# Opening stage of a transformer layer: value weights loaded by rows in eight chunks, first token tile in halves, products chunk by chunk

## The chip, the cores and the metric

One core of a Trainium2 chip runs one layer of a streaming-encoder trunk (1024 tokens, width 1024). The metric is the device time of one execution in microseconds (us), lower is better. Engines are named as in the profile: PE is TensorE (PEld its weight loads), DVE VectorE, ACT ScalarE, POOL GpSimd, SP SyncE, which issues all the DMA transfers here.

## What the kernel must compute

Only the start of the layer matters here: the normalised tokens `xn`, and the two value projections `va` and `vb` out of one combined input projection. The rest of the layer (attention, output projection, convolutional feed-forward, gate) follows unchanged.

```
def rms_norm(x, g):
    xf = x.astype(jnp.float32)
    y = xf * lax.rsqrt(jnp.mean(xf * xf, axis=-1, keepdims=True) + EPS)
    return (y * g.astype(jnp.float32)).astype(x.dtype)
...
        xn = rms_norm(h, norm_mix[i])
        proj = xn @ w_in[i]
        qa, ka, va, qb, kb, vb = jnp.split(proj, SPLITS, axis=-1)
...
        h = h + jnp.concatenate([oa, ob], axis=-1) @ w_out[i]
        h = h + gated_conv_ffn(rms_norm(h, norm_ffn[i]), w_ffn_in[i], conv_w[i], conv_b[i], w_ffn_out[i])
        gate = jax.nn.sigmoid(rms_norm(h, norm_ple[i]) @ w_ple_gate[i])
        h = h + gate * (p[i] @ w_ple[i])
    return rms_norm(h, norm_final)
```

The value columns are 512 of `vb` (from column 1792) and 128 of `va` (from column 640): 640 columns by 1024 rows of `w_in`, 2.5 MB.

## The kernel before

Every engine has its own program, written out by hand, and semaphores order them. Nothing is scheduled by a planner: the order on an engine is the order of the code in its block.

To keep float32 accuracy, every operand of a matrix product is split in two, `hi` (a rounded copy that ACT makes) and `lo` (the rest, which DVE makes by subtraction, L1185, after ACT's copy L793), and every product is made of three (`SPLIT3`: hi·hi, hi·lo, lo·hi).

The opening works on eight token tiles of 128 tokens, t = 0 to 7. For each, SP loads `x_in`; ACT squares it with a running sum (`square`, L796); DVE makes mean plus epsilon (L1194); POOL takes the power -0.5 (`power`, L687); DVE scales by that and by the gain `g_mix` into `xs0` (L1220); PE transposes `xs0` into PSUM in eight 128x128 pieces (`x_turn0`, L1729); ACT and DVE split the transposed tile into `act_t` (`x_hi0`, `x_lo0`); then PE makes the value products of the tile, 48 matmuls (`v_proj`, L1723: eight blocks k of 128 rows, times three, times two column pieces of 384 and 256). I call the tiles tile 0, tile 1 and so on, and "the products of tile u" is `v_proj(u)`.

The value weights come in five column pieces of 128 columns and all 1024 rows (`load_v`, five DMAs of 512 KB, in pieces of 512 bytes), into buffers that are not yet in use (`raws`). ACT and DVE split each (`split_v`) into `wv`. Since a piece of columns holds all rows, the products of tile 0 can begin on the first three column pieces (`v_proj(0, (0,))` waits for `wv_lo` 3) and go on with the other two (`v_proj(0, (1,))` waits for `wv_lo` 5). Before that PE runs transposes of the identity whose result nobody reads, 28 ahead of the transposes of tile 0 and 36 behind them.

SP's queue holds, in this order: `x_in` of tile 0, `g_mix`, the five weight loads, `x_in` of tile 1, the small tables (`prow` with the convolution's columns, `oneh` and `relb` for the bias table), six small constants, `x_in` of tile 2, the first query/key weight tile (`load_w(0)`, into `w_raw`, which is also the buffer of weight piece 2 and so waits for its split), and the other tiles. The small tables are turned by PE after tile 1's transposes (`cols_t`, `brow_t`) and copied by ACT after tile 0's value copies.

ACT's and DVE's loops run over t and hold at each t: the square (or scaling) of tile t, then, for t of 2 and more, the split of tile t - 1, then the value results of tile t - 2. At t = 0 they also hold the five weight splits and tile 0's split. ACT's square of tile 1 waits for `wv_lo` 4, because its junk output lies where weight piece 3 was landed.

Of the kernel before, what the change touches and what calls it, by code (L numbers as in the profile page):

```python
# [16 lines left out]
ALU = mybir.AluOpType  # L17
# [46 lines left out]
def build(nc, x, p, w_in, w_out, sinks, lambda_q, lambda_k, subln_gain, rel_bias, norm_mix, norm_ffn,  # L64
# [7 lines left out]
    def sb(stack, name, shape, dt=F32):  # L72
        return stack.enter_context(nc.sbuf_tensor(name, shape, dt))
# [3 lines left out]
    def sem(name):  # L77
# [20 lines left out]
    by_type = ExitStack()  # L98
    k_f = sb(by_type, "k_f", [P, 2, SEQ])
    by_type.close()  # L100
# [9 lines left out]
    g_mix = sb(early, "g_mix", [P, D])  # L110
    wv_raw = sb(early, "wv_raw", [P, 2, KD, P])
    prow = sb(early, "prow", [P, P])
# [19 lines left out]
    V_CUT = 3 * P  # L132
    raws = [wv_raw[:, 0], wv_raw[:, 1], w_raw[:, :, :],
            xs0[:, 1, :].rearrange("p (k n) -> p k n", k=KD), k_f[:, 0, :].rearrange("p (k n) -> p k n", k=KD)]
    q_a = wq[:, 4 * D:12 * D].rearrange("p (s l c u q) -> p s l c u q", s=2, l=2, c=NCH, u=2)
# [52 lines left out]
    def blk_there(eng, q, n):  # L188

        eng.wait_ge(wv_loaded[q], (16 if q < 5 else 0) + 16 * n)  # L190

# [212 lines left out]
    def _(sp):  # L404
        sp.dma_start(x_in[:, 0, :], x[0:P, :]).then_inc(x_loaded[0], 16)
        sp.dma_start(g_mix[:, :], row(norm_mix, D)).then_inc(S.gain_in, 16)

        def load_v(r):
            c = VB0 + P * r if r < 4 else VA0
            sp.dma_start(raws[r], w_in_v[:, :, c:c + P]).then_inc(wv_loaded[r], 16)  # L410

        load_v(0)
        load_v(1)
        load_v(2)
        load_v(3)
        load_v(4)
        sp.dma_start(x_in[:, 1, :], x[P:2 * P, :]).then_inc(x_loaded[1], 16)
# [10 lines left out]
        def load_w(j):  # L428
            if j == 0:
                sp.wait_ge(S.wv_lo, 3)  # L430
            else:
                sp.wait_ge(S.w_lo, j)
            at = 0
            for c, n in tiles[j]:
                sp.dma_start(w_raw[:, :, at:at + n], w_in_v[:, :, c:c + n]).then_inc(S.w_loaded, 16)
                at += n

        for t in range(2, NT):
            sp.wait_ge(S.xs0_ready, t - 1)
            sp.dma_start(x_in[:, t % 2, :], x[t * P:(t + 1) * P, :]).then_inc(x_loaded[t % 2], 16)  # L440
            if t == 2:
                load_w(0)

# [4 lines left out]
        load_w(2)  # L448
        sp.wait_ge(S.xs0_ready, NT)
        sp.wait_ge(S.tr0, NT)  # L450
        sp.wait_ge(S.wv_lo, 5)
        sp.wait_ge(S.consts_ready, 1)
# [338 lines left out]
    def _(act):  # L791
# [18 lines left out]
        def x_hi0(t):  # L810
            act.wait_ge(S.tr0, t + 1)
            b = 2 * (t % 2)
            copy(act_t[:, 0, :, t * P:(t + 1) * P], ps[:, b:b + 2, :].rearrange("p b (k n) -> p (b k) n", k=4), S.xhi0)

        for t in range(NT + 2):
            if t < NT:
                act.wait_ge(x_loaded[t % 2], 16 * (t // 2 + 1))
                if t == 1:
                    act.wait_ge(S.wv_lo, 4)
                if t >= 2:  # L820
                    act.wait_ge(S.tr0, t - 1)
# [17 lines left out]
            if t == 2:  # L839
                act.wait_ge(S.cols_t, 1)  # L840
                copy(cols[:, :], ps[:, 7, 0:4 * NF], S.act_self)
                act.wait_ge(S.brow_t, 1)
                copy(brow[:, :], ps[0:AH + BH, 5, 0:NREL], S.brow_ready)

# [330 lines left out]
    def _(dve):  # L1175
# [19 lines left out]

        def split_v(r):
            dve.wait_ge(S.wv_hi, r + 1)
            dst = wv[:, :, :, P * r:P * r + P]
            low(dst[:, 1], raws[r], dst[:, 0], S.wv_lo)

# [4 lines left out]
        def x_lo0(t):  # L1205
            dve.wait_ge(S.xhi0, t + 1)
            b = 2 * (t % 2)
            sl = slice(t * P, (t + 1) * P)
            low(act_t[:, 1, :, sl], ps[:, b:b + 2, :].rearrange("p b (k n) -> p (b k) n", k=4),
                act_t[:, 0, :, sl], S.xlo0)  # L1210

        for t in range(NT + 2):
            if t < NT:
                dve.wait_ge(S.sq0, t + 1)
                mean_eps(stat[:, 56 + t % 2:57 + t % 2], stat[:, t:t + 1], D, S.ms0)
            if t == 0:
                dve.wait_ge(S.gain_in, 16)
            if t < NT:
                dve.wait_ge(S.pow0, t + 1)
                nc.vector.scalar_tensor_tensor(out=xs0[:, t % 2, :], in0=x_in[:, t % 2, :],  # L1220
                                               scalar=stat[:, 8 + t:9 + t], in1=g_mix[:, :],
                                               op0=ALU.mult, op1=ALU.mult).then_inc(S.xs0_ready, 1)
            if t == 0:
                split_v(0)
                x_lo0(0)
                for r in range(1, 5):
                    split_v(r)
            if t == 5:
                split_w(0)
            if 2 <= t <= NT:  # L1230
# [490 lines left out]
    def _(pe):  # L1721
# [486 lines left out]
```

## Time and profile before

| | |
|---|---|
| runs of the kernel before | 1227.92, 1230.97, 1232.18 us; median 1230.97 |
| profiled execution, first to last instruction (span) | 1229.7 us, the one time that the profiled execution has |
| PE busy | 1197.1 us, 97% of the span |
| DVE, ACT, POOL busy | 867.3, 517.8, 250.2 us |
| mean granted TensorE clock | 0.992 of full speed |

The span runs from the first to the last instruction of one profiled execution; the runs are timed on the device without the profiler's records. The busy share is an average over the whole layer; what the opening costs is read from a timeline of its own. "PEclk" in the profile is the share of full speed that TensorE's clock was granted: 1.00 is 2.4 GHz, 0.50 is 1.2 GHz. Instruction times in the timeline are those of a group of like instructions that follow one another: its start, its length, and in brackets how long the engine had been idle and what ended that.

### The profile page before, as it was taken

Reading aid. Unit: us, or ns where it says so; the run is one execution under the profiler, and the core shown is the slowest. Engines: PE = TensorE matmul, PEld = TensorE weight load, DVE = VectorE, ACT = ScalarE, POOL = GpSimd, SP = SyncE. Lnnn points to the kernel's source line nnn. Section 1 sums busy time; section 2 is a strip of 40 time slices with the busy share of each in tenths; the row PEclk is TensorE's granted clock in tenths of the full one; section 3 lists DMA queues with packets and bytes.
Section 4 is the critical chain, followed back from the end, with each engine's and each line's share of the span. In section 5 each row is a group of like instructions: output and inputs, shape, how many; then the busy total and the mean of one; then the engine's idle time right before and its main releaser. Section 6 shows DMA issues by size and latency. Waiting matters only on the chain.

```text
span 1229.7 us, 17128 instructions
## 1 busy us (share of the span) xinstructions
PE 1197.1 (97%) x6167; PEld 1001.8 (81%) x6167; DVE 867.3 (71%) x1514; ACT 517.8 (42%) x1045; POOL 250.2 (20%) x291
## 2 busy tenths in 40 slices
PE   8999999999888999999999999999999999999997
PEld 7998887788676888888888888888888888888886
DVE  5433786877886577877787777877777999964443
ACT  4312665565655224433343343343344444733321
POOL 0000000344455122232332323323210000000000
PEclk9999999999899999999999999999999999999999
DMA  7464233111831512242322333233499533620101
GB/s 217 89 90 91 50 89 76 42 40 69 222 139 42 164 52 81 82 128 94 121 87 89 125 103 112 95 94 112 146 345 312 172 95 103 225 75 26 43 35 51
DMA packets 127916, 136.08 MB, mean 111 GB/s; under 512 B 15714, under 2 KB 93274, under 8 KB 127770
## 3 DMA queue, kind: packets, MB, share of 16 engines
q1 hardware_dynamic: 127834, 135.00, 36.1%
q8 instruction: 49, 0.80, 0.3%
q14 instruction: 33, 0.27, 0.1%
HBM read 96.77 MB, written 37.22 MB: 109 GB/s over the span
## 4 chain that ended last, share of the span: by engine, by line
PE 61%; issue 4%; DVE 2%; POOL 1%; ACT 1%; POOLq 0%; DVEq 0%; ACTq 0%
PE ps L1723 60%; PE ps L1729 1%; DVE xs L1474 1%; DVE h L1469 0%; DVE conv L1410 0%; POOL stat L687 0%; ACT xs L796 0%; DVE act_t L1185 0%; POOL stat L706 0%; POOL bias_a L712 0%; POOL more_f L714 0%; PE ps L2118 0%; ACT wbuf L793 0%; POOL o_t L709 0%; DVE h L1688 0%
## 5 line engine op out<-in xcount | busy, mean ns | idle before, releaser
L1723 PE MATMUL ps<-act_t,wbuf 128*128 128x512 f32 x1200 | 280.1, 389 | 0.5 <-DVE a_buf L1499 0.5
L1723 PEld LDWEIGHTS ps<-act_t,wbuf 128*128 128x128 f32 x1200 | 225.2, 188 | 47.5 <-DVE a_buf L1499 0.8
L1723 PE MATMUL ps<-wbuf 128*128 128x512 f32 x912 | 214.8, 390 | 0.0
L1723 PEld LDWEIGHTS ps<-wbuf 128*128 128x128 f32 x912 | 170.6, 188 | 35.1
L1723 PE MATMUL ps<-act_t,wq 128*128 128x512 f32 x624 | 152.2, 396 | 3.6 <-DVE wq L1187 3.0
L1723 PEld LDWEIGHTS ps<-act_t,wq 128*128 128x128 f32 x624 | 114.3, 188 | 30.8 <-issue 7.5
L687 POOL TENSOR_TENSOR stat<-stat 128x1 f32<-128x1 f32 x32 | 17.6, 549 | 420.9 <-DVE stat L1194 420.9
L793 ACT ACTIVATE wbuf<-raw 128x512 fp32r<-128x512 f32 (+1 forms) x107 | 69.0, 646 | 73.9 <-PE ps L1723 63.8
L1723 PE MATMUL ps<-hx,wbuf 128*128 128x512 f32 x408 | 95.7, 389 | 0.0
L1185 DVE TENSOR_TENSOR wbuf<-raw,wbuf 128x512 fp32r<-128x512 f32 (+1 forms) x107 | 87.4, 818 | 11.5 <-ACT wbuf L793 11.2
L1723 PEld LDWEIGHTS ps<-hx,wbuf 128*128 128x128 f32 x408 | 76.5, 188 | 15.9
L875 ACT ACTIVATE e_t<-ps,small 128x128 f32<-128x128 f32 (+7 forms) x64 | 47.3, 740 | 63.4 <-DVE small L1314 62.3
L793 ACT ACTIVATE wbuf<-xs 128x512 fp32r<-128x512 f32 x66 | 39.8, 624 | 71.9 <-DVE xs L1410 54.2
L1723 PE MATMUL ps<-wbuf,act_t 128*128 128x512 f32 x288 | 69.6, 395 | 0.0
L1723 PEld LDWEIGHTS ps<-wbuf,act_t 128*128 128x128 f32 x288 | 52.9, 188 | 10.5
L1723 PE MATMUL ps<-wq,act_t 128*128 128x384 f32 (+1 forms) x384 | 59.5, 315 | 1.5 <-DVE wq L1185 1.5
L1723 PEld LDWEIGHTS ps<-wq,act_t 128*128 128x128 f32 x384 | 57.9, 193 | 2.0 <-issue 1.7
L1723 PE MATMUL ps<-act_t,more 128*128 128x512 f32 x240 | 56.8, 389 | 0.0
L714 POOL TENSOR_TENSOR wbuf_f<-wbuf_f 128x512 f32<-128x512 f32 x33 | 52.2, 1581 | 18.6 <-DVE wbuf_f L1553 15.6
L1185 DVE TENSOR_TENSOR a_t<-ps,a_t 128x512 fp32r<-128x512 f32 (+4 forms) x64 | 44.6, 715 | 15.4 <-ACT a_t L793 15.3
L1723 PEld LDWEIGHTS ps<-act_t,more 128*128 128x128 f32 x240 | 45.0, 188 | 9.4
L1185 DVE TENSOR_TENSOR wbuf<-xs,wbuf 128x512 fp32r<-128x512 f32 x66 | 50.3, 762 | 0.5
(208 smaller groups left out, 1962.8 us busy)
## 6 DMA issues: line engine op xcount, KB each, us to landing
u_ops<-wbuf_f SPq DMA_DIRECT2D x77, 256.0 KB, 2.2
raw<-u_ops SPq DMA_DIRECT2D x77, 256.0 KB, 2.7
raw<-in_w_ffn_in SPq DMA_DIRECT2D x33, 512.0 KB, 3.8
g_ffn<-in_w_ffn_in SPq DMA_DIRECT2D x11, 512.0 KB, 3.9
act_f<-in_w_ffn_out SPq DMA_DIRECT2D x21, 256.0 KB, 4.3
w_raw<-in_w_in SPq DMA_DIRECT2D x10, 512.0 KB, 4.4
wbuf_f<-in_w_ffn_out SPq DMA_DIRECT2D x18, 256.0 KB, 5.9
x_in<-in_x SPq DMA_DIRECT2D x8, 512.0 KB, 3.8
```

The lines of the kernel that those rows point to most:

```text
L687: nc.gpsimd.tensor_tensor(dst, src, stat[:, 63:64], ALU.pow).then_inc(done, 1)
L714: nc.gpsimd.tensor_tensor(dst, a, b, ALU.subtract).then_inc(done, 1)
L793: nc.scalar.activation(dst, src, ACT.Copy, scale=scale).then_inc(done, 1)
L875: nc.scalar.activation(e_t[:, pr, m, 0:w], psf[:, at:at + w], ACT.Exp, scale=-1.0, bias=small[:, o + 2 + m:o + 3 + m], accum_out=small[:, ...
L1185: ins = nc.vector.tensor_tensor(dst, src, hi.bitcast(F32), ALU.subtract)
L1474: nc.vector.scalar_tensor_tensor(out=xs[:, i % 2, :], in0=h[:, t, :], scalar=stat[:, 8 + i:9 + i], in1=g_ffn[:, :], op0=ALU.mult, op1=ALU. ...
L1723: return nc.tensor.matmul(dst, lhs, rhs, start=start, stop=stop)
L1729: ins = nc.tensor.transpose(psf[:, bank * HALF + k * P:bank * HALF + (k + 1) * P], src[:, k * P:(k + 1) * P], ident[:, :])
```

## The change

The value weights are loaded by rows: eight chunks of 128 rows, each chunk in two DMAs (512 columns of `vb`, 256 KB, and 128 columns of `va`, 64 KB), into eight buffers of 640 columns (`v_raws`). The small tables move ahead of the weights in SP's queue, `x_in` of tile 1 stands between the second and the third chunk, and `x_in` of tile 2 stands right behind the last chunk, ahead of the six constants. `load_w(0)` no longer waits, since `w_raw` is no longer used for value weights.

ACT and DVE split chunk by chunk (640 columns instead of 1024, eight times instead of five). Tile 0 is scaled, transposed and split in two halves (`first_hi`, `first_lo`). Chunks 0 to 2 are split at t = 0 and chunks 3 to 7 at t = 1, behind tile 1's scaling; tile 1's split stands between those of chunks 5 and 6. The copies of the small tables move from t = 2 to t = 0 on ACT.

On PE 24 transposes of the identity stay and the 36 go; the small tables are turned before tile 0; the products of tile 0 run block by block, each waiting for its chunk, and tile 1's transposes stand ahead of block 6.

```diff
-    raws = [wv_raw[:, 0], wv_raw[:, 1], w_raw[:, :, :],
-            xs0[:, 1, :].rearrange("p (k n) -> p k n", k=KD), k_f[:, 0, :].rearrange("p (k n) -> p k n", k=KD)]
+    v_half = v_f[:, NT * 2 * P:2 * NT * 2 * P]
+    v_raws = [wv_raw[:, 0], wv_raw[:, 1]] + [x[:, NV * i:NV * (i + 1)] for x in (v_half, k_f) for i in range(3)]
...
-        def load_v(r):
-            c = VB0 + P * r if r < 4 else VA0
-            sp.dma_start(raws[r], w_in_v[:, :, c:c + P]).then_inc(wv_loaded[r], 16)
...
+        def load_v(k):
+            sp.dma_start(v_raws[k][:, 0:4 * P], w_in[k * P:(k + 1) * P, VB0:VB0 + 4 * P]).then_inc(wv_loaded[k], 16)
+            sp.dma_start(v_raws[k][:, 4 * P:NV], w_in[k * P:(k + 1) * P, VA0:VA0 + P]).then_inc(wv_loaded[k], 16)
...
+        load_v(0)
+        load_v(1)
+        load_x(1)
+        for k in range(2, KD):
+            load_v(k)
+        sp.wait_ge(S.xs0_ready, 2)
+        load_x(2)
...
             if t == 0:
                 split_v(0)
-                x_hi0(0)
-                for r in range(1, 5):
-                    split_v(r)
+                first_hi(0)
+                first_hi(1)
+                split_v(1)
+                act.wait_ge(S.cols_t, 1)
+                copy(cols[:, :], ps[:, 7, 0:4 * NF], S.act_self)
+                act.wait_ge(S.brow_t, 1)
+                copy(brow[:, :], ps[0:AH + BH, 5, 0:NREL], S.brow_ready)
+                split_v(2)
+            if t == 1:
+                split_v(3)
+                split_v(4)
+                split_v(5)
+                x_hi0(1)
+                split_v(6)
+                split_v(7)
...
-        def v_proj(u, cuts):
+        def v_proj(u):
+            cuts = (0, 1)
             for k in range(KD):
+                if u == 0:
+                    if k == 6:
+                        x_turn0(1)
+                    pe.wait_ge(S.wv_lo, k + 1)
+                    if k == 0:
+                        pe.wait_ge(S.xlo0, 1)
+                    if k == 4:
+                        pe.wait_ge(S.xlo0, 2)
...
-        for _ in range(28):
+        for _ in range(24):
             nc.tensor.transpose(ps[:, 7, 0:P], ident[:, :], ident[:, :])
-        x_turn0(0)
-        for _ in range(36):
-            nc.tensor.transpose(ps[:, 7, 0:P], ident[:, :], ident[:, :])
-        pe.wait_ge(S.xlo0, 1)
-        pe.wait_ge(S.wv_lo, 3)
-        v_proj(0, (0,))
-        pe.wait_ge(S.wv_lo, 5)
-        v_proj(0, (1,))
-        x_turn0(1)
         pe.wait_ge(S.cols_in, 32)
...
+        for half in range(2):
+            pe.wait_ge(S.xs0_ready, half + 1)
+            for k in range(4 * half, 4 * half + 4):
+                ins = nc.tensor.transpose(psf[:, k * P:(k + 1) * P], xs0[:, 0, k * P:(k + 1) * P], ident[:, :])
+            ins.then_inc(S.tr0, 1)
+        v_proj(0)
```

DVE's order changes as ACT's does. These are DVE's instructions in the kernel before, from the first mean (`TENSOR_SCALAR stat`) to the split of tile 1; `xs` is the scaled tile `xs0`, the rows that write `wq` are the weight splits (named by the buffer that they read), and those that write `act_t` the token splits.

```order
L1194 TENSOR_SCALAR stat<-stat 128x1 [waits sq0]
L1220 SCALAR_TENSOR_TENSOR xs<-x_in,stat,g_mix 128x1024 [waits pow0,gain_in]
L1185 TENSOR_TENSOR wq<-wv_raw,wq 128x8x128 [waits wv_hi]
L1185 TENSOR_TENSOR act_t<-ps,act_t 128x8x128 [waits xhi0]
L1185 TENSOR_TENSOR wq<-wv_raw,wq 128x8x128 [waits wv_hi]
L1185 TENSOR_TENSOR wq<-w_raw,wq 128x8x128 [waits wv_hi]
L1185 TENSOR_TENSOR wq<-xs,wq 128x8x128 [waits wv_hi]
L1185 TENSOR_TENSOR wq<-k_f,wq 128x8x128 [waits wv_hi]
L1194 TENSOR_SCALAR stat<-stat 128x1 [waits sq0]
L1220 SCALAR_TENSOR_TENSOR xs<-x_in,stat,g_mix 128x1024 [waits pow0]
```

And these are DVE's in the changed kernel, from the third weight split to the scaling of tile 2.

```order
L1199 TENSOR_TENSOR wq<-v_f,wq 128x640 [waits wv_hi]
L1208 TENSOR_SCALAR stat<-stat 128x1 [waits sq0]
L1244 SCALAR_TENSOR_TENSOR xs<-x_in,stat,g_mix 128x1024 [waits pow0]
L1199 TENSOR_TENSOR wq<-v_f,wq 128x640 [waits wv_hi] x2
L1199 TENSOR_TENSOR wq<-k_f,wq 128x640 [waits wv_hi]
L1199 TENSOR_TENSOR act_t<-ps,act_t 128x8x128 [waits xhi0]
L1199 TENSOR_TENSOR wq<-k_f,wq 128x640 [waits wv_hi] x2
L1208 TENSOR_SCALAR stat<-stat 128x1 [waits sq0]
L1244 SCALAR_TENSOR_TENSOR xs<-x_in,stat,g_mix 128x1024 [waits pow0]
```

Before, all weight splits stood ahead of tile 1's mean; now tile 1's mean and scaling stand in their middle, and tile 1's split (the row that writes `act_t`) stands between chunks 5 and 6, ahead of tile 2's scaling instead of behind it. On PE the kernel before had this order at the start (`ident` alone is the transposes that nobody reads; `prow` and `oneh,relb` are the small tables).

```order
L1753 MATMUL ps<-ident 128x128 x28
L1729 MATMUL ps<-ident,xs 128x128 x8
L1756 MATMUL ps<-ident 128x128 x36
L1723 MATMUL ps<-wq,act_t 128x384 x24
L1723 MATMUL ps<-wq,act_t 128x256 x24
L1729 MATMUL ps<-ident,xs 128x128 x8
L1764 MATMUL ps<-ident,prow 128x88
L1723 MATMUL ps<-oneh,relb 12x384
```

The changed kernel has this one; it stops at the first of tile 0's matmuls.

```order
L1794 MATMUL ps<-ident 128x128 x24
L1796 MATMUL ps<-ident,prow 128x88
L1755 MATMUL ps<-oneh,relb 12x384
L1802 MATMUL ps<-ident,xs 128x128 x8
L1755 MATMUL ps<-wq,act_t 128x384
```

The small tables stand ahead of tile 0 now, the 36 transposes are gone, and tile 1's transposes (not in these rows) stand behind 36 of tile 0's 48 matmuls.

## Rows read from the trace of the kernel before

**Rows 1.** The page's first part: span, and PE's busy time.

```profile
span 1229.7 us, 17128 instructions
...
PE 1197.1 (97%) x6167; PEld 1001.8 (81%) x6167; DVE 867.3 (71%) x1514; ACT 517.8 (42%) x1045; POOL 250.2 (20%) x291
```

**Rows 2.** Timeline of PE, 0 to 52 us.

```profile
1.54 5.31 PE L1753 MATMUL ps<-ident 128*128 128x128 f32 x28 [1.54 <-POOL ident L682]
...
14.40 7.30 PE L1723 MATMUL ps<-wq,act_t 128*128 128x384 f32 x48 [1.46 <-DVE wq L1185]
...
25.23 1.09 PE L1729 MATMUL ps<-ident,xs 128*128 128x128 f32 x8 [1.84 <-DVE xs L1220]
26.36 8.78 PE L1723 MATMUL ps<-wq,act_t 128*128 128x384 f32 x48
...
35.77 7.29 PE L1723 MATMUL ps<-wq,act_t 128*128 128x384 f32 x48
...
43.69 7.29 PE L1723 MATMUL ps<-wq,act_t 128*128 128x384 f32 x48
```

**Rows 3.** Timeline of ACT, DVE and POOL, 0 to 27 us.

```profile
4.49 1.06 ACT L796 ACTIVATE xs<-x_in 128x1024 f32<-128x1024 f32 x1 [2.49 <-DMA x_in<-in_x]
...
5.91 0.55 POOL L687 TENSOR_TENSOR stat<-stat 128x1 f32<-128x1 f32 x1 [4.42 <-DVE stat L1194]
...
6.57 1.28 DVE L1220 SCALAR_TENSOR_TENSOR xs<-x_in,stat,g_mix 128x1024 f32<-128x1024 f32 x1 [0.75 <-POOL stat L687]
...
8.31 1.06 ACT L793 ACTIVATE wq<-wv_raw 128x1024 fp32r<-128x1024 f32 x1 [2.68 <-DMA wv_raw<-in_w_in]
...
21.89 1.06 ACT L796 ACTIVATE xs<-x_in 128x1024 f32<-128x1024 f32 x1 [3.76 <-DMA x_in<-in_x]
...
22.95 1.00 ACT L793 ACTIVATE act_t<-ps 128x1024 fp32r<-128x1024 f32 x1
...
23.89 1.28 DVE L1220 SCALAR_TENSOR_TENSOR xs<-x_in,stat,g_mix 128x1024 f32<-128x1024 f32 x1 [0.66 <-POOL stat L687]
...
25.09 1.22 DVE L1185 TENSOR_TENSOR act_t<-ps,act_t 128x1024 fp32r<-128x1024 f32 x1
```

**Rows 4.** Timeline, 87 to 89 us: ACT's copy and DVE's split of 512 columns.

```profile
87.23 0.60 ACT L793 ACTIVATE k_a<-ps 128x512 fp32r<-128x512 f32 x1 [2.27 <-PE ps L1723]
87.86 0.69 DVE L1185 TENSOR_TENSOR k_a<-ps,k_a 128x512 fp32r<-128x512 f32 x1 [2.01 <-ACT k_a L793]
```

**Rows 5.** Transfers from 0 to 100 us: KB each, median us from issue to landing.

```profile
x_in<-in_x SPq DMA_DIRECT2D x8, 512.0 KB, 3.8
...
g_mix<-in_norm_mix SPq DMA_DIRECT2D x1, 512.0 KB, 5.3
...
lqk<-in_lambda_q SPq DMA_DIRECT2D x2, 32.0 KB, 4.0
```

**Rows 6.** SP's queue, 0 to 17 us: start and length of issues.

```profile
1.19 0.41 SPq L406 DMA_DIRECT2D g_mix<-in_norm_mix  x1
...
13.40 0.42 SPq L423 DMA_DIRECT2D lqk<-in_lambda_q  x1
...
16.23 0.43 SPq L440 DMA_DIRECT2D x_in<-in_x  x1
```

**Rows 7.** Stretches: length, busy us (x instructions) by engine, granted clock, DMA share, GB/s.

```profile
10.00:12.00 2.00, 2.00 (x20) 2.00 (x19) 2.00 (x3) 1.29 (x3) 0.00 (x0) 1.00 1.20 291
14.00:16.00 2.00, 1.60 (x9) 1.63 (x10) 1.43 (x2) 1.28 (x2) 0.00 (x0) 1.00 1.10 356
...
24.00:26.00 2.00, 0.77 (x7) 0.78 (x8) 2.00 (x2) 2.00 (x7) 0.00 (x0) 1.00 0.01 2
26.00:28.00 2.00, 1.96 (x9) 1.72 (x8) 1.34 (x6) 1.18 (x3) 0.55 (x1) 0.56 0.76 240
28.00:30.00 2.00, 2.00 (x11) 2.00 (x10) 2.00 (x2) 0.00 (x0) 0.00 (x0) 0.59 0.06 23
...
22.20:23.00 0.80, 0.80 (x7) 0.34 (x5) 0.00 (x0) 0.80 (x3) 0.00 (x0) 1.00 1.04 419
```

More of the change, by code:

```diff
@@ L39 @@
 QB0, KB0, VB0 = 768, 1280, 1792
+NV = 640
 HALF = 512
@@ L98, in build @@
     by_type = ExitStack()
-    k_f = sb(by_type, "k_f", [P, 2, SEQ])
+    k_f = sb(by_type, "k_f", [P, 2 * SEQ])
+    v_f = sb(by_type, "v_f", [P, 2 * NT * 2 * P])
     by_type.close()
@@ L110, in build @@
     g_mix = sb(early, "g_mix", [P, D])
-    wv_raw = sb(early, "wv_raw", [P, 2, KD, P])
+    wv_raw = sb(early, "wv_raw", [P, 2, NV])
     prow = sb(early, "prow", [P, P])
@@ L188, in blk_there @@
     def blk_there(eng, q, n):
-        eng.wait_ge(wv_loaded[q], (16 if q < 5 else 0) + 16 * n)
+        eng.wait_ge(wv_loaded[q], (32 if q < KD else 0) + 16 * n)
     def s_tmp(n, f):
@@ L406, in _ @@
         sp.dma_start(g_mix[:, :], row(norm_mix, D)).then_inc(S.gain_in, 16)
-        def load_v(r):
-            c = VB0 + P * r if r < 4 else VA0
-            sp.dma_start(raws[r], w_in_v[:, :, c:c + P]).then_inc(wv_loaded[r], 16)
[L412 to L417, printed above, removed]
         sp.dma_start(prow[0:3 * NF, :], conv_w.rearrange("c (f p) -> (c f) p", p=P)).then_inc(S.cols_in, 16)
@@ L421, in _, with load_x @@
         sp.dma_start(relb[:, :], rel_bias).then_inc(S.onehot_in, 16)
+        def load_v(k):
+            sp.dma_start(v_raws[k][:, 0:4 * P], w_in[k * P:(k + 1) * P, VB0:VB0 + 4 * P]).then_inc(wv_loaded[k], 16)
+            sp.dma_start(v_raws[k][:, 4 * P:NV], w_in[k * P:(k + 1) * P, VA0:VA0 + P]).then_inc(wv_loaded[k], 16)
+        def load_x(t):
+            sp.dma_start(x_in[:, t % 2, :], x[t * P:(t + 1) * P, :]).then_inc(x_loaded[t % 2], 16)
+        load_v(0)
[5 more added lines that the diff above has]
+        load_x(2)
         for j in range(2):
@@ L428, in load_w @@
         def load_w(j):
-            if j == 0:
-                sp.wait_ge(S.wv_lo, 3)
-            else:
+            if j >= 1:
                 sp.wait_ge(S.w_lo, j)
@@ L436, in load_w @@
                 at += n
[L438 to L442, printed above, removed]
+        load_w(0)
+        for t in range(3, NT):
+            sp.wait_ge(S.xs0_ready, t)
+            load_x(t)
         load_w(1)
@@ L448, in _ @@
         load_w(2)
-        sp.wait_ge(S.xs0_ready, NT)
-        sp.wait_ge(S.tr0, NT)
-        sp.wait_ge(S.wv_lo, 5)
+        sp.wait_ge(S.xs0_ready, NT + 1)
+        sp.wait_ge(S.tr0, NT + 1)
+        sp.wait_ge(S.wv_lo, KD)
         sp.wait_ge(S.consts_ready, 1)
@@ L796, in square, with split_v, first_hi @@
             nc.scalar.activation(junk, src, ACT.Square, accum_out=acc).then_inc(done, 1)
-        def split_v(r):
-            act.wait_ge(wv_loaded[r], 16)
-            copy(wv[:, 0, :, P * r:P * r + P], raws[r], S.wv_hi)
+        def split_v(k):
+            act.wait_ge(wv_loaded[k], 32)
+            copy(wv[:, 0, k, :], v_raws[k], S.wv_hi)
+        def first_hi(half):
+            act.wait_ge(S.tr0, half + 1)
+            copy(act_t[:, 0, 4 * half:4 * half + 4, 0:P], ps[:, half, :].rearrange("p (k n) -> p k n", k=4),
+                 S.xhi0)
         def split_w(j):
@@ L810, in x_hi0 @@
         def x_hi0(t):
-            act.wait_ge(S.tr0, t + 1)
+            act.wait_ge(S.tr0, t + 2)
             b = 2 * (t % 2)
@@ L817, in _ @@
                 act.wait_ge(x_loaded[t % 2], 16 * (t // 2 + 1))
-                if t == 1:
-                    act.wait_ge(S.wv_lo, 4)
                 if t >= 2:
-                    act.wait_ge(S.tr0, t - 1)
+                    act.wait_ge(S.tr0, t)
                 square(x_in[:, t % 2, :], xs0[:, t % 2, :], stat[:, 56 + t % 2:57 + t % 2], S.sq0)
@@ L824, in _ @@
                 split_v(0)
-                x_hi0(0)
-                for r in range(1, 5):
-                    split_v(r)
+                first_hi(0)
[13 more added lines that the diff above has]
+                split_v(7)
             if t == 5:
                 split_w(0)
-            if 2 <= t <= NT:
+            if 3 <= t <= NT:
                 x_hi0(t - 1)
@@ L838, in _ @@
                 copy(v_a[:, u, 0, :], ps[:, 6 + u % 2, P:2 * P], S.vhi)
[L839 to L843, printed above, removed]
         def unit_hi(u):
@@ L1194, in mean_eps, with split_v, first_lo @@
             nc.vector.tensor_scalar(dst, src, 1.0 / width, EPS, ALU.mult, ALU.add).then_inc(done, 1)
[L1196 to L1199, printed above, removed]
+        def split_v(k):
+            dve.wait_ge(S.wv_hi, k + 1)
+            low(wv[:, 1, k, :], v_raws[k], wv[:, 0, k, :], S.wv_lo)
+        def first_lo(half):
+            dve.wait_ge(S.xhi0, half + 1)
+            ks = slice(4 * half, 4 * half + 4)
+            low(act_t[:, 1, ks, 0:P], ps[:, half, :].rearrange("p (k n) -> p k n", k=4), act_t[:, 0, ks, 0:P],
+                S.xlo0)
         def split_w(j):
@@ L1205, in x_lo0 @@
         def x_lo0(t):
-            dve.wait_ge(S.xhi0, t + 1)
+            dve.wait_ge(S.xhi0, t + 2)
             b = 2 * (t % 2)
@@ L1217, in _ @@
                 dve.wait_ge(S.gain_in, 16)
-            if t < NT:
+                dve.wait_ge(S.pow0, 1)
+                for half in range(2):
+                    nc.vector.scalar_tensor_tensor(out=xs0[:, 0, HALF_X[half]], in0=x_in[:, 0, HALF_X[half]],
+                                                   scalar=stat[:, 8:9], in1=g_mix[:, HALF_X[half]], op0=ALU.mult,
+                                                   op1=ALU.mult).then_inc(S.xs0_ready, 1)
+            if 1 <= t < NT:
                 dve.wait_ge(S.pow0, t + 1)
@@ L1224, in _ @@
                 split_v(0)
-                x_lo0(0)
-                for r in range(1, 5):
-                    split_v(r)
+                first_lo(0)
+                first_lo(1)
+                split_v(1)
+                split_v(2)
+            if t == 1:
+                split_v(3)
+                split_v(4)
+                split_v(5)
+                x_lo0(1)
+                split_v(6)
+                split_v(7)
             if t == 5:
                 split_w(0)
-            if 2 <= t <= NT:
+            if 3 <= t <= NT:
                 x_lo0(t - 1)
@@ L1733, in x_turn0 @@
         def x_turn0(t):
-            pe.wait_ge(S.xs0_ready, t + 1)
+            pe.wait_ge(S.xs0_ready, t + 2)
             if t >= 2:
-                pe.wait_ge(S.xlo0, t - 1)
+                pe.wait_ge(S.xlo0, t)
             turn8(xs0[:, t % 2, :], 2 * (t % 2), S.tr0)
-        def v_proj(u, cuts):
+        def v_proj(u):
+            cuts = (0, 1)
             for k in range(KD):
+                if u == 0:
[6 more added lines that the diff above has]
+                        pe.wait_ge(S.xlo0, 2)
                 for n, (a, b) in enumerate(SPLIT3):
@@ L1766, in _ @@
         mm(ps[0:AH + BH, 5, 0:NREL], relb[:, :], oneh[:, :], True, True).then_inc(S.brow_t, 1)
+        for half in range(2):
+            pe.wait_ge(S.xs0_ready, half + 1)
[3 more added lines that the diff above has]
+        v_proj(0)
         for t in range(2, NT + 1):
@@ L1770, in _ @@
             u = t - 1
-            pe.wait_ge(S.xlo0, u + 1)
+            pe.wait_ge(S.xlo0, u + 2)
             if u == 1:
@@ L1776, in _ @@
                 pe.wait_ge(S.vlo, u - 1)
-            v_proj(u, (0, 1))
+            v_proj(u)
         def unit(u, part=None):
@@ L1783, in unit @@
                 if u == 0:
-                    pe.wait_ge(S.xlo0, NT)
+                    pe.wait_ge(S.xlo0, NT + 1)
                 if u < FIRST_UNITS:
```

## The prediction

> **What bounds the kernel now.** I read the page first: PE is busy for 1197.1 of 1229.7 us [rows 1], so nearly everything waits for PE, and time can be won only where PE is not at work or works slowly. PE's timeline of the opening came next [rows 2]. PE makes transposes that nobody reads until the weights are there, starts the products of tile 0 at 14.40 and those of tile 1 at 26.36, after an idle stretch of 1.84 us behind DVE. From tile 2 on it is in step: tile 2 starts at 35.77 and tile 3 at 43.69, 7.92 us apart, and ACT and DVE are idle for most of it. So all that the opening can win or lose is how much earlier or later **the products of tile 2 start than 35.77 us**. What follows is PE's own work and shifts as a whole.
>
> The clock is the third thing to see. Tile 1's products took 8.78 us, tile 2's 7.29 [rows 2]; the stretches show why: granted 1.00 at 24 to 26 us while PE idled, 0.56 and 0.59 in the next two [rows 7]. From 26.36 to 35.77 is 9.41 us instead of 7.92: this fall cost 1.5 us. The earlier gap, 1.46 us ahead of 14.40, was followed by a granted 1.00.
>
> Last, ACT's and DVE's timeline of the same place [rows 3] tells what PE waited for: `x_in` of tile 2, issued at 16.23 [rows 6], let its square start only at 21.89, 5.7 us later where the median of such loads is 3.8 [rows 5]; scaling followed at 23.89, PE's transposes at 25.23. Tile 1's split on DVE (25.09 to 26.31) ended just before tile 1's products.
>
> **The change, part by part.**
>
> *Transfers.* The bytes are the same, in larger pieces for four fifths of them. `g_mix` has landed by 1.19 + 5.3 = 6.5 us as before [rows 5, 6]. The small tables are 92 KB, 0.2 to 0.3 us at the rates below, so 6.8. Pieces of 512 bytes came at 291 GB/s (10 to 12 us), pieces of 4 KB at 419 (22.2 to 23.0) [rows 7]; the trace has no piece of 2 KB from HBM alone. A chunk of 328 KB is thus 0.78 to 1.13 us; I take 0.9, since a fifth of it is in the small pieces and the rest between. Chunk 0 is there at 7.7, chunk 1 at 8.6, tile 1 (512 KB, 1.25) at 9.9, chunks 2 to 7 at 10.8, 11.7, 12.6, 13.5, 14.4, 15.3, tile 2 at 16.6: 5 us sooner than it was. Issuing does not hold this up: 0.43 for each [rows 6], some 0.9 a chunk, and the first chunk's are out near 4 us.
>
> *Splits.* 1024 columns cost ACT 1.06 and DVE 1.22 [rows 3], 512 cost 0.60 and 0.69 [rows 4], so 640 cost about 0.71 and 0.82. Back to back each engine gives back about 0.1 of that (ACT's square at 21.89 of 1.06 and its accumulator's read are followed by the next copy at 22.95). Eight chunks are 8 x 0.72 = 5.8 us on DVE against 5 x 1.13 = 5.7: the work stays, its order changes.
>
> *The chain, step by step* (estimates from those rows; PE's part at full clock, 7.12 us between 35.77 and the next transposes, or 0.89 a block of six matmuls). Scaling of tile 0 begins at 6.57 as now, in halves of about 0.7, so it ends at 8.0. PE has the small tables turned by about 7.8, and tile 0's halves at 8.4 and 8.8. ACT: chunk 0 7.8 to 8.5, halves to 9.5, chunk 1 to 10.1, the two table copies to 10.6, chunk 2 10.9 to 11.6, square of tile 1 11.5 to 12.65, chunks 3, 4, 5 to 14.5. DVE: chunk 0 to 9.4, halves to 10.6, chunk 1 to 11.3, chunk 2 11.65 to 12.5; then tile 1's mean waits for the square (12.7), POOL's power takes it to 13.55 (0.66 from its start to the scaling [rows 3]), scaling to 14.8, chunks 3, 4, 5 to 15.6, 16.3, 17.05. PE: blocks 0, 1, 2 at 10.0, 11.35, 12.5; block 3 at 15.6, then 4 and 5 without a gap to 18.3.
>
> Here stands the new wait. Tile 1's transposes come behind block 5, and tile 1's split stands ahead of chunks 6 and 7 on ACT and DVE. Queued behind it are those two splits, and behind them tile 2's square, mean and scaling; PE waits for all of these in turn. From the end of block 5: transposes 1.05, ACT's copy 1.0 [rows 3], DVE's subtraction 1.22, two chunks 1.5, mean and power 0.8, scaling 1.3, transposes until the first product 0.9: 7.8 us, plus about 0.1 for handing over. In that time PE has two blocks and two sets of transposes to do, 3.9 us. So tile 1's products start at 18.3 + 7.9 = 26.2 and tile 2's at 34.1, **if the clock holds**. Against 35.77 that is 1.65 us won.
>
> *The clock.* It won't hold, I think. Blocks 0 to 2 come with gaps, and from 13.4 to 15.6 PE is idle for 2.2 us: longer than the 1.84 that was followed by the fall, while 1.46 was not. The 36 transposes that kept PE at work are gone. If the fall comes near 16 us and ends with block 4, blocks 3 to 5 end at 19.85 instead of 18.3 (half speed, as in 26 to 30 us [rows 7]: block 4 costs 1.6 to 1.8 instead of 0.89), and all behind them moves by 1.55: tile 1 at 27.75, tile 2 at 35.7. Against 35.77 that is nothing. What the change wins, the 1.5 us of slow clock in tile 1 and the late `x_in` of tile 2, it gives back in the chain that PE now waits for and in a slow clock one tile sooner.
>
> *The rest.* `load_w(0)` without its wait, `cols` and `brow` sooner: all were ready long before their users, so nothing. The small constants come later by the one load of tile 2 and are read only after tile 7's values. Blocks of tile 0 in another order of the same 48 matmuls: nothing.
>
> **The sum.** -1.65 + 1.55 = -0.1 us at tile 2. The profiled span of 1229.7 becomes 1229.6; the runs' median is 1230.97, so 1.3 us more than that profile, which I keep: **1230.9 us**, no change. The three runs shown lie 4.3 us apart, and about 0.3% (3.7 us) is what a measurement can tell from none.
>
> **The rivals.**
>
> *The clock holds* (or falls where no product stands): tile 2 at 34.1, 1229.3 us; still within 0.3%. For it speaks that PE was granted 1.00 after a gap of 1.46 and that blocks 0 to 2 are some work; against it the 2.2 us. A floor beneath it: DVE's work from 6.57 on with no wait but the chain above, 1.35 + 0.75 + 1.25 + 1.45 (tile 0, three chunks) + 0.85 + 1.2 (tile 1's scaling) + 2.2 (three chunks) + 3.0 (block 5, transposes, copy) + 1.15 + 1.5 + 0.85 + 1.2 + 0.9, ends at 24.2, so tile 2 at 32.1 at best: 3.7 us won, 1227.3 us. Only this floor would count as faster, and it needs early chunks, tile 1's square ahead of chunk 2, and a full clock at once.
>
> *The clock falls twice or stays low* (the other side: slower). PE is idle again between tile 1's transposes and block 6, 3 us (20.9 to 24.0), and half idle until tile 1. A second fall that reaches tile 1's transposes costs about what it cost before, 1.4 us: 1232.4. If the clock is low throughout from 16.0 until tile 1 has begun: blocks 3 to 5 end at 20.6, both sets of transposes cost 2 us instead of 1, and tile 1 starts at 30.5 with 1.5 us of slow products, so tile 2 at 39.9: 4.1 us lost, 1235.1. It decides at block 5: if that and tile 1's transposes still run at the low clock, slower it is. The Trainium skill's page "TensorE: Matmul & The Clock Gate", section "HAM oscillation — how this bites in real kernels", says that bursts of matmuls with waits for data between them fall back to half clock burst after burst. By that rule this is the likely case; the trace agrees with one fall after a wait, and shows no series of them here.
>
> *Chunks later.* At 1.13 us a chunk, chunk 2 comes at 11.4 and chunk 5 at 14.8; the square of tile 1 and all behind it move by 0.6, the rest is hidden behind DVE: 1231.5. Were transfers served one at a time, each for the 3.7 to 4.0 us of small ones, sixteen of them would put chunk 5 past 45 us and the kernel past 1255. Against it: the 32 KB loads are issued 0.5 apart and land within 4.0 [rows 5, 6]. The skill's "DMA: Bandwidth & Descriptors", section "Rules for kernel authors", asks for 1 MiB a transfer and calls those under 64 KB mostly overhead; by it 64 KB and 256 KB instead of 512 KB speak against this change. The trace shows overhead that overlaps.
>
> **How the numbers follow.** One fall, nothing won: 0.4. Clock holds, or nearly: 0.25. A second fall, or later chunks (1231.5 to 1232.4): 0.2. Low throughout (1235): 0.07. The floor (1227.3): 0.07. Transfers in series: 0.01. Together faster by over 0.3% 0.09, slower 0.11, the rest between, with the runs' own spread of some 2 us either way on top. The range of 8 in 10 takes the floor and the low clock nearly in: 1227.5 to 1234.5.
>
> **What would show it.** In the changed kernel's trace: chunk splits on ACT at 7.8 and then never late for data after chunk 2; DVE idle about 3 us between chunk 5 and tile 1's split; PE idle before block 3 and between tile 1's transposes and block 6; granted clock 0.5 near 16 to 19 us; tile 2's products at 34 to 37 us. Wrong it would be if tile 2 starts before 32.5 (a chain shorter than I worked out), after 39 (clock or transfers), or if the time moves elsewhere: the clock's other falls in the middle of the kernel may shift with it, which I put at nothing.

## The result, and the profile after

| | before | after |
|---|---|---|
| median of 9 runs each, us | 1229.29 (1227.69 to 1232.18) | 1232.88 (1229.94 to 1235.13) |
| ratio, 95% interval | | 1.0024 [1.0012, 1.0035] |
| span of the profiled execution, us | 1229.7 | 1230.0 |
| products of tile 2 start (profiled execution), us | 35.77 | 37.49 |

The change costs 0.24%, some 3 us. I had forecast no change. The page's first part has the same shape as before [rows 1]:

```profile
span 1230.0 us, 17068 instructions
...
PE 1192.8 (97%) x6127; PEld 996.9 (81%) x6127; DVE 868.8 (71%) x1519; ACT 517.8 (42%) x1049; POOL 249.6 (20%) x291
```

PE's timeline of the opening, which answers to [rows 2] (start, length, group, idle time before it):

```profile
10.41 3.49 PE L1755 MATMUL ps<-wq,act_t 128*128 128x384 f32 x18 [1.07 <-DVE act_t L1199]
15.81 4.45 PE L1755 MATMUL ps<-wq,act_t 128*128 128x384 f32 x18 [1.91 <-DVE wq L1199]
20.10 1.03 PE L1761 MATMUL ps<-ident,xs 128*128 128x128 f32 x8
24.23 3.57 PE L1755 MATMUL ps<-wq,act_t 128*128 128x384 f32 x12 [3.10 <-DVE wq L1199]
27.60 1.91 PE L1761 MATMUL ps<-ident,xs 128*128 128x128 f32 x8
29.16 7.70 PE L1755 MATMUL ps<-wq,act_t 128*128 128x384 f32 x48
...
37.49 7.29 PE L1755 MATMUL ps<-wq,act_t 128*128 128x384 f32 x48
...
45.41 7.29 PE L1755 MATMUL ps<-wq,act_t 128*128 128x384 f32 x48
```

The first row is blocks 0 to 2 of tile 0 (18 of 48 matmuls), the second blocks 3 to 5, the third tile 1's transposes, the fourth blocks 6 and 7. Two things are to be seen: PE is idle for 3.10 us ahead of block 6, waiting for DVE; and the twelve matmuls behind it, which take 2.03 us in a kernel further down, took 3.57. The stretches say why (columns as in [rows 7]; the clock is the third number from the right):

```profile
10.00:12.00 2.00, 1.47 (x8) 1.24 (x9) 1.72 (x4) 2.00 (x6) 0.00 (x0) 1.00 1.07 382
...
14.00:16.00 2.00, 0.19 (x1) 0.19 (x2) 2.00 (x3) 0.77 (x2) 0.00 (x0) 1.00 1.07 372
16.00:18.00 2.00, 2.00 (x10) 2.00 (x10) 1.23 (x2) 0.00 (x0) 0.00 (x0) 0.60 1.04 242
18.00:20.00 2.00, 2.00 (x10) 2.00 (x9) 0.00 (x0) 0.00 (x0) 0.00 (x0) 0.54 0.93 320
20.00:22.00 2.00, 1.13 (x10) 0.89 (x8) 0.00 (x0) 0.83 (x1) 0.00 (x0) 1.00 0.04 16
22.00:24.00 2.00, 0.00 (x0) 0.00 (x0) 1.77 (x2) 2.00 (x4) 0.00 (x0) 0.81 0.00 0
24.00:26.00 2.00, 1.76 (x6) 1.77 (x7) 1.34 (x4) 0.48 (x2) 0.55 (x1) 0.50 0.00 0
26.00:28.00 2.00, 2.00 (x9) 2.00 (x9) 0.93 (x1) 0.16 (x1) 0.00 (x0) 0.50 0.11 16
28.00:30.00 2.00, 2.00 (x11) 2.00 (x10) 1.11 (x4) 2.00 (x6) 0.04 (x1) 0.50 0.71 254
```

Each of PE's two idle stretches (before block 3, before block 6) brings a fall of the clock: to 0.60 and 0.54 in the first case, to 0.50 in the second. The second sets in while PE is still idle (0.81 at 22 to 24 us) and lasts into tile 1's products. DVE's timeline shows what PE waited for:

```profile
16.41 0.82 DVE L1199 TENSOR_TENSOR wq<-k_f,wq 128x640 fp32r<-128x640 f32 x1
22.23 1.23 DVE L1199 TENSOR_TENSOR act_t<-ps,act_t 128x1024 fp32r<-128x1024 f32 x1 [5.00 <-ACT act_t L797]
23.37 1.55 DVE L1199 TENSOR_TENSOR wq<-k_f,wq 128x640 fp32r<-128x640 f32 x2
```

Chunk 5's split ends at 17.2; then DVE stands still for 5.00 us, since the next in its order is tile 1's split, which needs ACT's copy, which needs PE's transposes, which stand behind block 5. Chunks 6 and 7 (the last row), long landed, wait behind it.

### The profile page after: what moved, and what is told of

Same layout as the page of the kernel before. It is cut to its first block, busy times and chain, and to the rows that moved or that the text cites. A ratio compares the mean times of both kernels' runs of the same rounds, so it can differ in the third digit from the quotient of the medians.

```text
span 1230.0 us, 17068 instructions
## 1 busy us (share of the span) xinstructions
PE 1192.8 (97%) x6127; PEld 996.9 (81%) x6127; DVE 868.8 (71%) x1519; ACT 517.8 (42%) x1049; POOL 249.6 (20%) x291
## 4 chain that ended last, share of the span: by engine, by line
PE 61%; issue 4%; DVE 2%; POOL 1%; ACT 1%; POOLq 0%; DVEq 0%; ACTq 0%
PE ps L1755 60%; PE ps L1761 1%; DVE xs L1506 1%; DVE h L1501 0%; DVE conv L1442 0%; POOL stat L691 0%; ACT xs L800 0%; DVE act_t L1199 0%; POOL stat L710 0%; POOL bias_a L716 0%; POOL more_f L718 0%; PE ps L2156 0%; ACT wbuf L797 0%; POOL o_t L713 0%; DVE conv L1717 0%
## 5 line engine op out<-in xcount | busy, mean ns | idle before, releaser
L797 ACT ACTIVATE wbuf<-xs 128x512 fp32r<-128x512 f32 x66 | 39.9, 624 | 71.6 <-DVE xs L1442 54.2
L1755 PE MATMUL ps<-wq,act_t 128*128 128x384 f32 (+1 forms) x384 | 62.6, 323 | 6.2 <-DVE wq L1199 5.0
```

Of the source, the lines that this page charges most:

```text
L797: nc.scalar.activation(dst, src, ACT.Copy, scale=scale).then_inc(done, 1)
L1755: return nc.tensor.matmul(dst, lhs, rhs, start=start, stop=stop)
```

## The experiments

Each kernel was timed in rounds against the kernel before on the same chip. "Tile 2" below is where the products of tile 2 start in that kernel's own profiled execution.

**before_again: the kernel before, again** (no edit).

> The kernel before, unchanged, so that its executions are seen more than once. Theory 1 (the profiled execution of before was a late one): here the products of tile 2 start at 32.5 to 34.5 us instead of 35.77, with no fall of the clock at 26 us, and the ratio is 1.000. Theory 2 (that profile was typical, and the changed kernel loses by its own later start alone): tile 2 starts at 35.5 to 36.0 again.

Ratio 0.9997 [0.9986, 1.0009], profiled span 1227.3. PE's timeline:

```profile
14.44 7.27 PE L1723 MATMUL ps<-wq,act_t 128*128 128x384 f32 x48 [1.51 <-DVE wq L1185]
...
24.14 1.09 PE L1729 MATMUL ps<-ident,xs 128*128 128x128 f32 x8 [0.74 <-DVE xs L1220]
25.28 7.31 PE L1723 MATMUL ps<-wq,act_t 128*128 128x384 f32 x48
...
33.22 7.29 PE L1723 MATMUL ps<-wq,act_t 128*128 128x384 f32 x48
```

And ACT's square of tile 2:

```profile
20.80 1.06 ACT L796 ACTIVATE xs<-x_in 128x1024 f32<-128x1024 f32 x1 [2.45 <-DMA x_in<-in_x]
```

Theory 1 holds. Tile 1's products took 7.31 us, not 8.78, and tile 2 starts at 33.22, 2.55 us sooner than in [rows 2]. The load of tile 2 let its square start at 20.80 instead of 21.89 [rows 3], PE's idle gap was 0.74 instead of 1.84, and no fall followed. The spans of all executions say which of the two profiles is the typical one: over the 67 later executions of the kernel before, the median is 1227.3 us, this profile's own, and only 7 reach the 1229.7 of the first.

**before_x2_sooner: the kernel before with tile 2's load ahead of the small constants.**

```diff
+        sp.wait_ge(S.xs0_ready, 1)
+        sp.dma_start(x_in[:, 0, :], x[2 * P:3 * P, :]).then_inc(x_loaded[0], 16)
         for j in range(2):
             sp.dma_start(lqk[:, j], row(lambda_q[j], HD)).then_inc(S.consts_in, 16)
```

(Further down, the loop that issued it before leaves it out.)

> The kernel before with one edit: tile 2's load stands ahead of the six small constants, as in the changed kernel. Theory 1 (the late landing at 21.9 us and the fall of the clock behind it were a chance of that one execution): ratio 0.999 to 1.001. Theory 2 (the late landing is there in most executions): tile 1's products start at 24.5 to 25.2 without a fall of the clock, tile 2's near 33, ratio 0.997 to 0.999.

Ratio 0.9995 [0.9986, 1.0004]; tile 2 at 32.89:

```profile
32.89 7.28 PE L1726 MATMUL ps<-wq,act_t 128*128 128x384 f32 x48
```

That is 0.3 us ahead of the typical execution above, and the interval of the ratio holds no change. The start of tile 2 alone would fit both theories; the ratio is theory 1's. Together with the 67 spans above it says that the late landing was that one execution's, not the kernel's.

**after_again: the changed kernel, again** (no edit).

> The changed kernel, unchanged, so that its clock is seen a second time. Theory 1 (the two falls come in nearly every execution): granted 0.50 somewhere between 16 and 30 us and the products of tile 2 at 36 to 38 us again, ratio 1.002 to 1.003. Theory 2 (they were a chance of that execution, as the fall of before was): tile 2 at 34.1 to 35.0, ratio then still 1.001 to 1.003 over all runs.

Ratio 1.0036 [1.0024, 1.0048], and tile 2 still later, at 38.26. PE's timeline of it, and the row of ACT's that tells why:

```profile
17.03 5.17 PE L1755 MATMUL ps<-wq,act_t 128*128 128x384 f32 x18 [1.91 <-DVE wq L1199]
22.00 1.28 PE L1761 MATMUL ps<-ident,xs 128*128 128x128 f32 x8
26.38 3.34 PE L1755 MATMUL ps<-wq,act_t 128*128 128x384 f32 x12 [3.10 <-DVE wq L1199]
...
30.34 7.29 PE L1755 MATMUL ps<-wq,act_t 128*128 128x384 f32 x48
...
38.26 7.29 PE L1755 MATMUL ps<-wq,act_t 128*128 128x384 f32 x48
```

```profile
12.32 0.74 ACT L797 ACTIVATE wq<-v_f 128x640 fp32r<-128x640 f32 x1 [1.42 <-DMA v_f<-in_w_in]
```

Theory 1 as far as two profiles can show it: the gaps (1.91 and 3.10 us) are the same and the low clock is there again, in blocks 3 to 5 (5.17 us instead of 2.9 with a full clock further down) and 6 and 7. Tile 2 and the ratio even lie above what I expected of it. Chunk 2 came late as well: ACT waited 1.42 us for it, and block 3 starts 1.22 us later than in the first profile. Tile 2 is only 0.77 us later, since here the clock was full again for tile 1's products (7.29 us instead of 7.70).

**warm_gaps: the changed kernel with PE kept at work in its gaps.**

```diff
+                    if k == 3:
+                        pe.wait_ge(S.act_self, 1)
+                        for _ in range(14):
+                            nc.tensor.transpose(ps[:, 7, 0:P], ident[:, :], ident[:, :])
                     if k == 6:
                         x_turn0(1)
+                        for _ in range(24):
+                            nc.tensor.transpose(ps[:, 7, 0:P], ident[:, :], ident[:, :])
```

> The changed kernel with 14 transposes of the identity ahead of block 3 and 24 ahead of block 6 of tile 0, where PE sat idle. Theory 1 (its two falls of the clock are the loss against its own chain): granted 1.00 from 16 to 30 us, tile 2's products at 33.8 to 34.6 us instead of 37.49, about 3 us less than the changed kernel and within 0.15% of before. Theory 2 (the chain of tile 1's split, chunks 6 and 7 and tile 2's scaling is the loss, the clock hidden behind it): tile 2 at 36.5 or later, ratio to before still 1.002 or more.

Ratio 1.0012 [1.0002, 1.0023]. PE's timeline:

```profile
13.95 1.69 PE L1778 MATMUL ps<-ident 128*128 128x128 f32 x14
16.01 2.91 PE L1755 MATMUL ps<-wq,act_t 128*128 128x384 f32 x18 [0.37 <-DVE wq L1199]
...
22.90 2.03 PE L1755 MATMUL ps<-wq,act_t 128*128 128x384 f32 x12 [0.49 <-DVE wq L1199]
...
34.42 7.29 PE L1755 MATMUL ps<-wq,act_t 128*128 128x384 f32 x48
```

Theory 1 in the mechanism: the granted clock is 1.00 throughout from 8 to 36 us, blocks 3 to 5 take 2.91 us instead of 4.45, blocks 6 and 7 2.03 instead of 3.57, and tile 2 starts at 34.42. But of the 3 us that I expected over all runs only about half go, 1.0024 to 1.0012, and the two intervals overlap. The rest is not the clock: with a full clock the chain still puts tile 2 1.2 us behind the 33.22 of a typical execution before.

**turn_sooner: the changed kernel with tile 1's transposes ahead of block 3.**

```diff
-                    if k == 6:
+                    if k == 3:
                         x_turn0(1)
```

> The changed kernel with one edit: tile 1's transposes stand ahead of block 3 instead of block 6. Theory 1 (the place of these transposes makes the chain that PE waits for): DVE's 5.0 us of idle time ahead of tile 1's split shrinks below 0.5, tile 1's products start near 23 and tile 2's at 30.5 to 32.5, ratio to before 0.996 to 0.999. Theory 2 (the wait only moves, to chunks 6 and 7 behind that split): tile 2 at 35 or later, ratio 1.001 to 1.003.

Ratio 0.9985 [0.9976, 0.9994]: one number moved, and the loss is a gain. PE's timeline, and the row of DVE's that had 5.00 us in brackets:

```profile
15.84 1.09 PE L1761 MATMUL ps<-ident,xs 128*128 128x128 f32 x8 [1.18 <-DVE xs L1244]
16.68 2.89 PE L1755 MATMUL ps<-wq,act_t 128*128 128x384 f32 x18
20.04 2.03 PE L1755 MATMUL ps<-wq,act_t 128*128 128x384 f32 x12 [0.47 <-DVE wq L1199]
...
31.55 7.29 PE L1755 MATMUL ps<-wq,act_t 128*128 128x384 f32 x48
```

```profile
18.03 1.22 DVE L1199 TENSOR_TENSOR act_t<-ps,act_t 128x1024 fp32r<-128x1024 f32 x1
```

Theory 1. The transposes fit into the gap that PE had ahead of block 3, where they wait 1.18 us for tile 1's scaling; DVE goes on to tile 1's split without a stop; and with shorter gaps the clock stays full (2.89 and 2.03 us for the blocks). Tile 2 starts at 31.55.

**split_last: the changed kernel with tile 1's split behind chunks 6 and 7.**

```diff
                 split_v(5)
-                x_hi0(1)
                 split_v(6)
                 split_v(7)
+                x_hi0(1)
```

(and the same on DVE with `x_lo0(1)`.)

> The changed kernel with tile 1's split behind the splits of chunks 6 and 7 on ACT and DVE instead of ahead of them; PE's order stays. Theory 1 (the loss is that chunks 6 and 7 are queued behind a split that waits for PE): DVE has no idle time between chunks 5 and 7, blocks 6 and 7 follow tile 1's transposes at once, tile 2 at 32.5 to 33.3 with a full clock (34.3 with one fall), ratio 0.999 to 1.0005. Theory 2 (tile 2's scaling behind tile 1's split is the loss, wherever the chunks stand): tile 2 at 34 or later with a full clock, ratio 1.001 or more.

Ratio 1.0019 [1.0010, 1.0027]. PE's timeline:

```profile
16.25 4.37 PE L1755 MATMUL ps<-wq,act_t 128*128 128x384 f32 x18 [1.91 <-DVE wq L1199]
...
21.33 2.01 PE L1755 MATMUL ps<-wq,act_t 128*128 128x384 f32 x12
25.96 1.09 PE L1761 MATMUL ps<-ident,xs 128*128 128x128 f32 x8 [2.62 <-DVE xs L1244]
26.80 7.29 PE L1755 MATMUL ps<-wq,act_t 128*128 128x384 f32 x48
...
34.72 7.29 PE L1755 MATMUL ps<-wq,act_t 128*128 128x384 f32 x48
```

Neither theory as I put it. Blocks 6 and 7 follow tile 1's transposes at once, as theory 1 said; but then PE waits 2.62 us for tile 2's scaling, which is still behind tile 1's split. The wait has only moved. This execution had one fall (blocks 3 to 5 took 4.37 us, some 1.5 too long), so by my estimate tile 2 would have been near 33.2 with a full clock, level with before. Set beside turn_sooner, this says that what counts most is when PE makes the transposes; which of DVE's jobs is queued behind them matters less.

The wait of 2.62 us shows one thing more. It is longer than the 1.91 us that were followed by a fall in the same execution, and yet no fall followed it: the transposes behind it took 1.09 us and tile 1's products 7.29, and the clock (columns as before) was 1.00:

```profile
24.00:26.00 2.00, 0.04 (x1) 0.05 (x1) 1.38 (x2) 1.42 (x5) 0.55 (x1) 1.00 0.00 0
```

The length of a gap alone does not decide whether the clock falls.

**before_no36: the kernel before without its 36 unread transposes.**

```diff
-        for _ in range(36):
-            nc.tensor.transpose(ps[:, 7, 0:P], ident[:, :], ident[:, :])
```

> The kernel before without its 36 unread transposes behind tile 0's: that part of the change alone. Theory 1 (they hold the clock): a fall between 12 and 17 us, tile 0's products 1.4 to 2.5 us longer than 7.3, tile 2 at 34.3 to 36, ratio 1.0005 to 1.002. Theory 2 (they do nothing, as PE has the tables and tile 0 to work on soon enough): tile 2 near 33.2, ratio 0.999 to 1.001.

Ratio 1.0007 [0.9998, 1.0016], tile 2 at 34.74:

```profile
14.41 9.14 PE L1723 MATMUL ps<-wq,act_t 128*128 128x384 f32 x48 [5.31 <-DVE wq L1185]
...
34.74 7.28 PE L1723 MATMUL ps<-wq,act_t 128*128 128x384 f32 x48
```

```profile
12.00:14.00 2.00, 0.00 (x0) 0.00 (x0) 1.88 (x2) 1.25 (x2) 0.00 (x0) 0.50 1.20 290
14.00:16.00 2.00, 1.59 (x5) 1.62 (x6) 1.43 (x2) 1.28 (x2) 0.00 (x0) 0.50 1.10 355
```

PE idle for 5.31 us, clock at 0.50, tile 0's products 9.14 us instead of 7.27: this is what the 36 bought. The profile shows theory 1; the interval of the time just reaches 1, so the size over all runs, 0.9 us, is not settled.

**turn_sq_sooner: the changed kernel with tile 1 sooner still**: transposes ahead of block 2, and tile 1's square and scaling ahead of chunk 2's split and the table copies.

```diff
-                split_v(2)
             if t == 1:
+                split_v(2)
                 split_v(3)
...
-                    if k == 6:
+                    if k == 2:
                         x_turn0(1)
```

(and on ACT the two table copies go behind chunk 2's split.)

> The changed kernel with tile 1's transposes ahead of block 2, and tile 1's square and scaling ahead of chunk 2's split and the table copies on ACT and DVE. Theory 1 (the chain through tile 1 sets the start of tile 2, so each part of it that is begun sooner counts): tile 2 at 29.8 to 30.6 us, 1 to 1.7 us ahead of the kernel with the transposes ahead of block 3, ratio 0.9965 to 0.998. Theory 2 (DVE's own work, back to back from 14.5 us on, sets it already): tile 2 at 31.2 or later, ratio 0.998 to 0.999.

Ratio 0.9971 [0.9960, 0.9983], median 1226.42 against 1229.38. PE's timeline:

```profile
13.56 1.09 PE L1761 MATMUL ps<-ident,xs 128*128 128x128 f32 x8 [1.19 <-DVE xs L1244]
14.41 3.77 PE L1755 MATMUL ps<-wq,act_t 128*128 128x384 f32 x24
...
21.96 7.29 PE L1755 MATMUL ps<-wq,act_t 128*128 128x384 f32 x48
...
29.89 7.29 PE L1755 MATMUL ps<-wq,act_t 128*128 128x384 f32 x48
```

Theory 1: tile 2 at 29.89, 1.66 us ahead of the one with block 3, and faster than both kernels of this study's start. All parts of the change are in it; only tile 1 stands elsewhere.

## Why the prediction was wrong

Nine profiles side by side:

| kernel | tile 2 starts, us | ratio to before |
|---|---|---|
| turn_sq_sooner | 29.89 | 0.9971 |
| turn_sooner | 31.55 | 0.9985 |
| before_x2_sooner | 32.89 | 0.9995 |
| before_again | 33.22 | 0.9997 |
| warm_gaps | 34.42 | 1.0012 |
| split_last | 34.72 | 1.0019 |
| before_no36 | 34.74 | 1.0007 |
| the change | 37.49 | 1.0024 |
| the change again | 38.26 | 1.0036 |

The first profile of the kernel before, 35.77, is not in the table: the ratios stand for many runs, and it is the unlike one.

**What bounds the kernel: right.** The time follows the start of tile 2's products through the nine, though not exactly: a ratio stands for many runs and a start for one, and what lies behind the start took from 1192.4 us (turn_sq_sooner) to 1195.1 (turn_sooner).

**Transfers and splits: nearly right.** 372 and 382 GB/s where the trace of before has 291 [rows 7], so the larger pieces came faster, within the bounds given; chunk 0's split on ACT began at 7.92 (forecast 7.8), and 640 columns took DVE 0.82 as worked out. The Trainium skill's "DMA: Bandwidth & Descriptors" ("Rules for kernel authors") asks for 1 MiB or more a transfer. The trace does not show that rule deciding: sixteen transfers of 256 and 64 KB moved more bytes a second than five of 512 KB, and four fifths of their bytes came in longer contiguous pieces; the size of a transfer alone was not tried. Chunk 2, which I had at 10.8, came late in four of the six profiles of kernels with chunks: ACT waited 0.75 to 1.42 us for it, and its split began at 11.31 to 12.32 (in the first profile at 11.11, without a wait for data).

**The chain: right to a quarter of a microsecond in the first profile.** Block 3 at 15.81 (forecast 15.6), tile 1's transposes at 20.10 (19.85, with the fall), block 6 at 24.23 (24.0), and the wait that took the others' place is the one named: tile 1's split ahead of chunks 6 and 7. With a full clock, in warm_gaps, tile 2 came at 34.42, where I had 34.1.

**The clock: the first fall right, the second only a rival.** I gave one fall 0.4, and the second fall together with later chunks 0.2. Both profiles of the change have a low clock twice. The second fall was priced at 1.4 us; tile 2 came at 37.49 against 35.7, 1.8 us later. That I had the first fall right is luck in part: I argued from the length of the gap, and the 2.62 us in split_last show that the length does not decide alone. The Trainium skill's "TensorE: Matmul & The Clock Gate", section "HAM oscillation — how this bites in real kernels", tells of a kernel whose bursts of matmuls wait for data in between and in which every burst starts at the low clock. The trace agrees here for two waits, the 1.91 and the 3.10 us, and not for the 2.62 us.

**The step that failed** is the one behind "Against 35.77 that is nothing": I took one profiled execution for the kernel. Its late load of tile 2 (1.1 us) and its fall of the clock (1.5 us) made 35.77; a second profile, with the median span, says 33.22. I had seen the sign (5.7 us to landing where the median is 3.8) and booked both as cost that the change would save. Nor were 1.3 us between that span and the median what lies around a span: over 67 later executions of before it is 2.03 to 2.13 us, so the profiled one would have been some 1231.8 against a median of 1229.3. Put right, the sum I called -0.1 us reads 35.7 - 33.2 = +2.5 with one fall and 37.5 - 33.2 = +4.3 with two; measured are 3.0 us (1.0024). It was the reference that was mis-sized, by 2.55 us, more than any term of the change; the second fall, 1.8 us, comes next. That the forecast of 1230.9 lies only 2.0 us below the measured 1232.88 is luck in part: it started from the median of three runs, 1230.97, and nine runs have 1229.29.

**How the 3 us split.** In warm_gaps, whose profile has a full clock, the ratio is 1.0012: some 1.5 us that the clock does not explain, of which the chain is 1.2 (34.42 against 33.22). A small part lies outside the span: 2.09 to 2.51 us around it for the fifteen executions of the change, mean 2.33, against 2.08 before. Such a quarter of a microsecond is in all five kernels with chunks, and no run here tells what it is. What is left for the clock is 1.5 us by the change's 1.0024, and some 3 by the 1.0036 of its second timing; it is not known better than that. How often the falls come is open: two profiles of the change have them, and of two of before one has a single fall.

**The other rivals.** The floor (tile 2 at 32.1) was one for this order of the program, and no profile of the change came near it. With the same parts in another order turn_sooner and turn_sq_sooner went beneath it, to 31.55 and 29.89, and the latter won 3.6 us (0.0029 of 1229.4). Low throughout (39.9) did not come either, though the second profile, at 38.26, was not far from it.

## What to carry to other kernels

Before pricing a change against one profiled execution, look for what in it is unlike its own pattern (a load that took 5.7 us where its like take 3.8), and price against the pattern, not against the accident. When weights arrive in pieces, the next tile's first step (here its transposes) belongs into the wait for the early pieces, not behind them: a short job that a whole chain hangs on should go where its engine would be idle. And work that nobody reads can be worth its place: taking it out left a gap, and in the profile the clock fell, though what that costs over all runs is not settled here (1.0007, with an interval that reaches 1).

## What the runs showed that I had not expected

The clock falls later too, in the middle of the kernel, and not in every execution of the same kernel. This is one stretch of the changed kernel's first profile (columns as before):

```profile
324.00:330.00 6.00, 4.03 (x30) 3.40 (x31) 5.86 (x15) 3.73 (x10) 3.33 (x6) 1.00 1.03 308
```

And the same stretch of its second:

```profile
324.00:330.00 6.00, 5.12 (x30) 4.50 (x28) 5.69 (x13) 3.96 (x10) 3.08 (x6) 0.53 1.03 282
```

Granted 1.00 in the one, 0.53 in the other. What lies behind tile 2's start took 1230.0 - 37.49 = 1192.5 us in the first and 1232.4 - 38.26 = 1194.1 in the second. These 1.6 us, half of what this study was about, come and go without any change to the kernel; that the clock alone makes them was not tried.
